# A two-layer hybrid trunk on one core: weights loaded and accumulated in halves of a unit, 47 instead of 55 accumulations, 137 units split whole, a new order of the items, zero matmuls at the first gate

## What is computed

```
x += 1/2 * (silu(h @ w1) * (h @ w3)) @ w2        # h = RMSNorm(x)
P  = RMSNorm(x) @ W_in                           # one projection for all branches
A: retention, 4 heads;  B: window attention, 16 q / 2 kv heads;  C: attention into 256 memory tokens
y  = sum_b sigmoid(gate_b) * (branch_b @ W_up_b);  x += y @ W_o
x += 1/2 * (silu(h @ w1') * (h @ w3')) @ w2'     # h = RMSNorm(x)
```

## Time and profile before

| what | value |
|---|---|
| median of three executions | 1435.11 us (1435.1 to 1437.61) |
| the profiled execution | 1435.34 us |
| its span, first to last instruction | 1433.5 us |
| mean granted TensorE clock | 0.997 |
| PE, DVE, ACT, POOL busy | 99%, 84%, 69%, 4% |
| DMA | 336.14 MB, mean 234 GB/s |

### The profile page before, as it was taken

How to read it: one execution, slowest core, us unless ns; L and a number is a source line. 1 busy time by engine, 2 the same in 40 slices (tenths; PEclk the granted TensorE clock), 3 DMA queues, 4 the chain that set the end, 5 groups by cost and what they waited for, 6 DMA issues and landing times.

```text
span 1433.5 us, 17418 instructions
## 1 busy us (share of the span) xinstructions
PE 1415.2 (99%) x6630; PEld 1161.0 (81%) x6630; DVE 1205.6 (84%) x1423; ACT 982.2 (69%) x1438; POOL 63.3 (4%) x88
## 2 busy tenths in 40 slices
PE   8999999999999999999999999999999999999997
PEld 6788888877878888888888888887778788888886
DVE  7999756889899868899889997468998898699885
ACT  6677666878766748676577675667786766576773
POOL 0000000000100000000000000000001000000000
PEclk9999999999999999999999999999999999999999
DMA  9799448787777576889749767468878765857971
GB/s 369 235 268 291 189 157 289 226 240 209 217 227 256 185 294 245 240 272 276 247 155 285 247 195 263 171 241 261 237 208 223 250 220 187 322 151 250 314 225 44
DMA packets 48675, 336.14 MB, mean 234 GB/s; under 512 B 5488, under 2 KB 6128, under 8 KB 8528
## 3 DMA queue, kind: packets, MB, share of 16 engines
q1 hardware_dynamic: 37536, 259.80, 48.4%
q0 software_dynamic: 8192, 58.59, 21.5%
q10 hardware_dynamic: 2864, 16.64, 2.9%
HBM read 327.67 MB, written 7.34 MB: 234 GB/s over the span
## 4 chain that ended last, share of the span: by engine, by line
PE 89%; DVE 6%; DMA 2%; ACT 1%; issue 1%; SPq 0%; POOLq 0%; POOL 0%; DVEq 0%; ACTq 0%
PE bank L815 27%; PE bank L818 27%; PE bank L816 27%; PE bank L876 3%; DVE w_lo L1671 3%; DMA raw<-in_stream 2%; PE bank L1170 1%; PE bank L1149 1%; PE bank L1031 1%; PE bank L1045 1%; ACT w_hi L1250 1%; DVE raw_x L1663 1%; PE bank L1060 1%; DVE raw_q L1663 0%; DVE w_lo_more L1671 0%
## 5 line engine op out<-in xcount | busy, mean ns | idle before, releaser
L1671 DVE TENSOR_TENSOR w_lo<-raw,w_hi 128x1024 fp32r<-128x1024 f32 x328 | 386.2, 1221 | 104.3 <-ACT w_hi L1250 103.9
L1250 ACT ACTIVATE w_hi<-raw 128x1024 fp32r<-128x1024 f32 x328 | 328.5, 1054 | 141.0 <-PE bank L818 115.5
L815 PE MATMUL bank<-w_hi,hT_lo 128*128 128x512 f32 (+1 forms) x640 | 251.4, 393 | 3.3 <-ACT stA L1489 1.6
L818 PE MATMUL bank<-w_lo,hT_hi 128*128 128x512 f32 (+1 forms) x640 | 246.2, 385 | 0.0
L816 PE MATMUL bank<-w_hi,hT_hi 128*128 128x512 f32 (+1 forms) x640 | 246.1, 384 | 0.0
L815 PE MATMUL bank<-w_hi,S_lo 128*128 128x512 f32 x400 | 158.8, 397 | 0.9 <-ACT snap L1338 0.9
L818 PE MATMUL bank<-w_lo,S_hi 128*128 128x512 f32 x400 | 155.9, 390 | 0.0
L816 PE MATMUL bank<-w_hi,S_hi 128*128 128x512 f32 x400 | 155.9, 390 | 0.0
L815 PEld LDWEIGHTS bank<-w_hi,hT_lo 128*128 128x128 f32 x640 | 120.3, 188 | 32.0 <-issue 4.0
L818 PEld LDWEIGHTS bank<-w_lo,hT_hi 128*128 128x128 f32 x640 | 120.3, 188 | 24.4
L816 PEld LDWEIGHTS bank<-w_hi,hT_hi 128*128 128x128 f32 x640 | 120.5, 188 | 22.3
(11 more groups left out here) (232 smaller groups left out, 2529.6 us busy)
## 6 DMA issues: line engine op xcount, KB each, us to landing
raw<-in_stream SPq DMA_DIRECT2D x154, 1024.0 KB, 5.5
raw_b<-in_stream SPq DMA_DIRECT2D x35, 1024.0 KB, 6.9
raw_q<-in_stream SPq DMA_DIRECT2D x33, 1024.0 KB, 7.7
raw<-in_stream POOLq DMA_DIRECT2D x24, 1024.0 KB, 8.7
raw_x<-in_stream SPq DMA_DIRECT2D x16, 1024.0 KB, 5.2
raw_b<-in_stream POOLq DMA_DIRECT2D x10, 1024.0 KB, 10.8
raw_q<-in_stream POOLq DMA_DIRECT2D x9, 1024.0 KB, 9.0
raw_a<-in_stream SPq DMA_DIRECT2D x6, 1024.0 KB, 5.1
```

What stands on the lines that cost most here:

```text
L815: nc.tensor.matmul(dst, xl, wh[:, a:b], start=first, stop=False, skip_group_check=more)
L818: return nc.tensor.matmul(dst, xh, wl[:, a:b], start=False, stop=last, skip_group_check=more)
L1250: nc.scalar.activation(slots(o)[0][:, part], raw_slot(s)[:, part], ACT.Copy).then_inc(hi_split, 1)
L1671: nc.vector.tensor_tensor(lo[:, part], raw_slot(s)[:, part], hi[:, part].bitcast(F32), ALU.subtract)\
```

## The change

1. **Halves.** Each load by SP is two DMAs of 512 KB, and each slot has two semaphores. Where the slot becomes free with the end of a split, the first half is issued one count of `weights_made` earlier (`SPLIT_ENDS`), when the first half of the old unit has been split. Each accumulation by POOL is two DMAs too. ACT waits for each half by itself (`raw_there`).
2. **ADDED** has 47 sums in place of 55, and DVE makes 65 in place of 57.
3. **WHOLE** was empty. Now 137 of the 328 units that are split at L1250 and L1671 in either layer are copied and subtracted with one instruction of 128x2048 (the list has 162 entries, of which 25 name no item).
4. **The order tables** are new. PE's matmuls on weights stay the same in number and shape.
5. **warm** issues 8 matmuls of zeros (128x512) on PE into the bank of the first gate's transposes, once that bank is free and before PE waits for `act_g`.

```diff
-mk0.1+xt0 mk1.0+xt1 mk1.1 S_sum S_hi skv.0 S_lo sq1.0 sq0.0 sq0.1 mkt sq1.1 skt mv0.0 sqt rk:1 rk:5 s0 mv0.1
...
-gs:7 ro gs:4 mq:5 mq:1 us0.1 mq:3 re mq:6 us1.0 mq:2 mq:7 us1.1 mq:4 gr:1 mqt gr:5 rt mkT_in mv_in gr:3 gr:6
+gs:7 ro gs:4 mq:5 re us0.1 mq:1 mq:3 mq:6 us1.0 mq:7 mq:2 mq:4 us1.1 gr:1 mqt gr:5 rt mkT_in gr:3 gr:6 mv_in
...
 FFN_ORDER = {(0, 1): """
-u0.0 u0.1 u1.0 g0 u1.1 p0:1 d0 g1 p0:5 p0:3 p0:6 p0:2 d1 p0:7 p1:5 p0:4 g3 p1:3 p1:1 d3 p1:6 g2 p1:2 d2 p1:7
+u0.0 u0.1 u1.0 g0 u1.1 p0:1 d0 p0:5 p0:3 p0:6 g1 p0:2 d1 p0:7 p1:5 p0:4 g3 p1:3 p1:1 d3 p1:6 g2 p1:2 d2 p1:7
...
 """.split(), (1, 1): """
-u0.0 u0.1 u1.0 g0 p0:1 u1.1 d0 p0:5 p0:3 p0:6 g1 p0:2 p0:7 p1:5 d1 g3 p0:4 p1:3 p1:1 d3 p1:6 g2 p1:2 p1:7 p2:5
+u0.0 u0.1 p0:1 u1.0 g0 u1.1 d0 p0:5 g1 p0:3 p0:6 p0:2 p0:7 p1:5 d1 p0:4 g3 p1:3 p1:1 d3 p1:6 g2 p1:2 p1:7 d2
...
-S_AFTER = {(0, 1): (0, 0, 3, 0, 4, 4), (0, 2): (0, 1, 2, 0, 3, 5), (1, 1): (0, 2, 3, 0, 3, 3), (1, 2): (0, 2, 2, 1, 2, 5)}
+S_AFTER = {(0, 1): (0, 3, 3, 0, 3, 4), (0, 2): (0, 1, 1, 0, 2, 4), (1, 1): (0, 2, 3, 0, 2, 4), (1, 2): (2, 2, 2, 2, 3, 4)}
...
-    (0, 2, 1): (6, 7, 4), (0, 2, 2): (7,), (0, 2, 3): (6, 7), (0, 0, 'rk'): (7, 4), (0, 0, 'rg'): (6, 7, 4),
-    (0, 0, 'gs'): (6, 7), (0, 0, 'mq'): (6, 7, 4), (0, 0, 'gr'): (7,), (0, 0, 'gm'): (7,), (1, 1, 0): (7, 4),
+    (0, 2, 1): (6, 7), (0, 2, 2): (6, 7), (0, 2, 3): (7,), (0, 0, 'rk'): (7,), (0, 0, 'rg'): (6, 7, 4),
+    (0, 0, 'gs'): (7,), (0, 0, 'mq'): (6, 7), (0, 0, 'gr'): (7,), (0, 0, 'gm'): (7,), (1, 1, 0): (7, 4),
...
             for o, unit, s, (until, owner), _ in loads[EARLY:]:
                 if until > 0:
-                    sp.wait_ge(weights_made, until)
+                    sp.wait_ge(weights_made, until - (until in SPLIT_ENDS))
...
-                sp.dma_start(raw_slot(s), stream[unit]).then_inc(raw_loaded[s], 16)
+                for n, part in enumerate(PARTS):
+                    if n and until > 0 and until in SPLIT_ENDS:
+                        sp.wait_ge(weights_made, until)
+                    sp.dma_start(raw_slot(s)[:, part], stream[unit, :, part]).then_inc(raw_loaded[s][n], 16)
...
+                    for h, part in enumerate(PARTS):
+                        pool.wait_ge(raw_loaded[to[0]][h], 16 * to[1])
...
+                        pool.dma_start(raw_slot(to[0])[:, part], stream[l * NU + quarter_unit(f, k, SUMS[m]), :, part], accum_op=ALU.add)\
...
                     if c == 0 and (l, f) == (0, 1):
                         pe.wait_ge(x0_copied, 2)
+                        pe.wait_ge(*room(l, f"gt{f}_{c}"))
+                        warm(8, where[l][f"gt{f}_{c}"][0])
...
                 if whole(o):
+                    raw_there(1)
                     nc.scalar.activation(slots(o)[0][:, :], raw_slot(s)[:, :], ACT.Copy).then_inc(hi_split, 2)
                     return
-                for part in PARTS:
+                for n, part in enumerate(PARTS):
+                    if n:
+                        raw_there(1)
```

More of the change, by code:

```diff
@@ L510, in sem @@
             return ctx.enter_context(nc.semaphore(name))
-        raw_loaded = [sem(f"raw_loaded{s}") for s in range(RAW_A + 1)]
+        raw_loaded = [[sem(f"raw_loaded{s}_{n}") for n in range(2)] for s in range(RAW_A + 1)]
         hi_split, weights_made, unit_used = sem("hi_split"), sem("weights_made"), sem("unit_used")
@@ L515, in build @@
         S_step, x0_copied = sem("S_step"), sem("x0_copied")
-        quarter_added = {m: [sem(f"quarter_added{m}_{n}") for n in range(2)] for m in (5, 6, 7, 4)}
+        quarter_added = {m: [[sem(f"quarter_added{m}_{n}_{h}") for h in range(2)] for n in range(2)] for m in (6, 7, 4)}
         x_stored, x_back, mkT_stored, mkT_back, mv_stored, mv_back = map(
@@ L614, in pair_no, with sum_ready @@
             return l * (len(PAIRS[1]) + len(PAIRS[2])) + (f - 1) * len(PAIRS[1]) + k
-        def sum_ready(l, pair, k):
+        def sum_ready(l, pair, k, h):
             if k in added(l, pair):
                 turn, count = (added_at[l, pair, k] - 1) % 2, (added_at[l, pair, k] + 1) // 2
-                return quarter_added[k][turn], 16 * count
+                return quarter_added[k][turn][h], 16 * count
             return weights_made, sum_at[l, pair, k]
@@ L676, in x_part @@
                 sp.dma_start(x[:, :, cols], x_in[:, cols].rearrange("(t p) d -> p t d", p=P)).then_inc(x_loaded[n], 16)
+            SPLIT_ENDS = {v for v in lo_at if v}
             x_part(0)
@@ L735, in add_quarters @@
                     to = raw_of[l, pair, WEIGHT[m]]
-                    pool.wait_ge(raw_loaded[to[0]], 16 * to[1])
-                    if behind:
-                        pool.wait_ge(weights_made, behind)
                     _, f, k = pair
-                    pool.dma_start(raw_slot(to[0]), stream[l * NU + quarter_unit(f, k, SUMS[m])], accum_op=ALU.add)\
-                        .then_inc(quarter_added[m][(added_at[l, pair, m] - 1) % 2], 16)
+                    for h, part in enumerate(PARTS):
+                        pool.wait_ge(raw_loaded[to[0]][h], 16 * to[1])
+                        if behind:
+                            pool.wait_ge(weights_made, behind)
+                        pool.dma_start(raw_slot(to[0])[:, part], stream[l * NU + quarter_unit(f, k, SUMS[m]), :, part], accum_op=ALU.add)\
+                            .then_inc(quarter_added[m][(added_at[l, pair, m] - 1) % 2][h], 16)
             def quarters_after(l, i):
@@ L790, in _, with warm @@
                 pe.nop().then_inc(psum_free[b], 1)
-            def warm(n):
+            def warm(n, b=0):
                 for _ in range(n):
-                    nc.tensor.matmul(ps[0][:, :], still[:, 0:P], still[:, :], start=True, stop=True)
+                    nc.tensor.matmul(ps[b][:, :], still[:, 0:P], still[:, :], start=True, stop=True)
             pe.wait_ge(still_ready, 1)
@@ L1237, in split, with raw_there @@
                 s, loads_so_far = loaded(o)
-                if item[0] == "prod" and item[3] in SUMS:
-                    act.wait_ge(*sum_ready(l, item[:3], item[3]))
-                else:
-                    act.wait_ge(raw_loaded[s], 16 * loads_so_far)
+                def raw_there(h):
+                    if item[0] != "prod" or item[3] not in SUMS:
+                        act.wait_ge(raw_loaded[s][h], 16 * loads_so_far)
+                    elif item[3] in added(l, item[:3]) or h == 0:
+                        act.wait_ge(*sum_ready(l, item[:3], item[3], h))
+                raw_there(0)
                 if slot_before[o] >= 0:
@@ L1658, in split @@
                     to, plus = (raw_of[o // NI, pair, q] for q in (WEIGHT[m], SUMS[m]))
-                    dve.wait_ge(raw_loaded[to[0]], 16 * to[1])
-                    dve.wait_ge(raw_loaded[plus[0]], 16 * plus[1])
+                    for n in range(2):
+                        dve.wait_ge(raw_loaded[to[0]][n], 16 * to[1])
+                        dve.wait_ge(raw_loaded[plus[0]][n], 16 * plus[1])
                     if sum_behind[o // NI, pair, m]:
```

27 lines of the change are left out of this document (14 added, 13 removed), and 8 rows, old and new, of the table ADDED.

## The result

The change makes the kernel slower: the median is 1448.26 us (1445.98 to 1450.04, four executions) against 1435.11, a ratio of 1.0087 with a 95% interval of 1.0075 to 1.0099. 1430.7 was forecast. The profiled execution took 1449.13 us, its span is 1447.3.

The account below looks back on a forecast made before the run. PE, busy 99%, was taken as the bound, with DVE limiting the first 70 us. Terms -1.65 - 2.1 - 0.9 - 0.4 - 0.2 + 0.6 = -4.65 gave 1430.7 us; 8-in-10 range 1428.2 to 1434.8.

Parts of the forecast that it names:

- loads and accumulations in halves: All transfers: less load on the queues and no PE wait for loads after 70 us; 0, bounds -0.5 and +1 us.
- The margin at us0.1: Narrowest place for DVE's added sums: first half of w_lo ready 0.5 us before PE takes it up.
- Whole splits: DVE: one full instruction replaces a pair of half splits, 0.07 us saved each; nine in the first 70 us give -0.6.
- one such place: A stall like that possible at us0.1, where a whole split comes 1.2 us later; +0.6 us, bounds 0 and +3.
- The mixing stages: Both layers: gr:1 finds bank 0 free, -2.1 us; rt's wait for `mqT` goes, -0.9 us.
- if something else is late there, 0: Upper bound of the gr:1 term in the mixing stage: the -2.1 us gain could come to nothing.
- rival 2: Only part holds: full DVE in the mixing stage brings waits back, 1433.2 us; or start fails, 1432.4; 0.21 shared with another rival.
- Rival 3: Slower: six DVE sums come due in the mixing stages, 1.7 us each, 10.2 in all, 1440.9 us; chance 0.09.
- The signs: Prediction wrong if PE waits over some 2 us for w_lo/w_hi after 70, p0:4 starts before 67.5, or whole-split cost differs clearly.
- The start: DVE's chain up to 70 us: earlier first half, whole splits and no idle for `act_b`, -1.65 us at p0:4.
- The zero matmuls: First gate: they hold the clock up, but DVE ends this stretch; 0, bounds 0 and -1.7 us.
- Rival 1: Start: the whole clock loss is won too, 1.7 us more, giving 1429.0 us; chance 0.20.

Follow-up runs that it names:

- all_one: The changed kernel with each load and each accumulation one DMA of 1 MB again; 1433.31 us, ratio 0.9982.
- all_one_no_whole: The changed kernel with loads and accumulations of 1 MB and an empty list of whole splits; 1431.93 us, ratio 0.9981.
- all_one_added55: The changed kernel with loads and accumulations of 1 MB and the 55 accumulations of the kernel before in place of 47; 1435.11 us, ratio 0.9999.
- before_warm: The kernel before with only the eight zero matmuls at the first gate added; 1435.49 us, ratio 1.0002.
- acc_rows: The kernel before with each accumulation in two DMAs of 512 KB cut by rows (64 rows of 8192 bytes), loads of 1 MB; 1453.10 us, ratio 1.0122.
- ffn_load_halves: The kernel before with the new order, sums and S_AFTER of the FFNs, the zero matmuls and loads in halves; 1432.93 us, ratio 0.9977.
- acc_one: The changed kernel with each of the 47 accumulations one DMA of 1 MB again, loads still in halves; 1437.72 us, ratio 1.0016.
- before_load_halves: The kernel before, with its tables and accumulations of 1 MB, and only the loads in halves; 1433.39 us, ratio 0.9991.

## Why the prediction was wrong

**The step that failed** is the one on loads and accumulations in halves: "PE waits for no load after 70 us, as the waits show, so I take 0. Bounds: -0.5 and +1". It is worth +15 us between all_one and the changed kernel, the share of the whole splits with late transfers included. By the ratios the loss is made up so: the new tables and the zero matmuls, with transfers of 1 MB and no whole split, gain 2.7 us; loads in halves then cost 4.2, accumulations in halves 4.3, and whole splits on top 6.7. In the tables of before, accumulations in halves cost 4.3 us as well on top of loads in halves, but loads in halves gained 1.3. So the new tables lose nothing by themselves and yet have a part in the loss, through the loads. Two things were wrong in the step. It took the cost of a transfer from the engines' time for its bytes; with 8 accumulations fewer that falls. But what counts is when the last half lands, and that is 2.4 us later at the median over all 55 (8.9 to 11.3 us, same tables). It goes with the traffic beside it: of the five accumulations in each of these two kernels beside which the other queues carried under 0.1 MB, the median went from 8.1 us only to 8.4. At 43.6 us the second half of the changed kernel lands 8.3 us after the first issue, as the whole did at 44.1. And it read from the list of waits that there is room, where the list only says that the room is not negative. The margin at us0.1, 0.5 us, stood in the prediction, but as one against added sums.

**Whole splits** were counted as -0.07 us each. Their price per instruction is right (2.28 to 2.29 us at L1681 from start to end, 2.20 from start to start in DVE's chain, and PE's loss is nothing clear with accumulations of 1 MB), but they cost 7 us together with late accumulations. The prediction priced the 1.2 us that the first half comes later, and then counted one such place.

**The mixing stages**, -2.1 and -0.9 us, failed as well. In layer 0 the new order with transfers of 1 MB gains 0.4 us from rg:7 to gr:2, and in layer 1 0.1. These are one execution's; in that of all_one_no_whole the same stretches lose 1.9 and gain 2.1. The wait for bank 0 does go, as forecast, and so does most of that for `mqT`. What I named as the bound "if something else is late there, 0" was the case: DVE, 90% busy, gives its combinations later, and PE waits at mq:7, mq:2 or mq:4 instead. The prediction itself had this as rival 2, with a split as what PE would wait for instead.

**Rival 3** (9%) named the right stages and the right sign, but its 1440.9 us is 7 us short, and its cause is not borne out: with transfers of 1 MB, taking eight sums back from DVE gains nothing (all_one_added55). Beside transfers in halves this wasn't run. So the 9% were on the right side by luck more than by their reason.

**The signs.** One of the prediction's signs of being wrong came: PE waits for `w_lo` after 70 us for 2.4 us in all (1.9 at L1681, 0.5 at L1686), against "some 2". It is the smaller part: of the 5.4 us for `gates` 4.1 are the two stops at gr:7 behind late accumulations, which no sign named.

**What held.** The start: -1.65 us were forecast at p0:4, -1.45 measured, with the forecast waits for `S_lo` (about 1.1; 1.0 measured, between starts less 0.23) and `gT2_lo` (1.4; 1.3) inside the stretch. p0:4 starts at 68.69 us (about 68.3 forecast). Nine splits up to there are whole, as counted; in the rows of Place 2 it is two pairs that become single, not three. The zero matmuls: 0, with the clock at 1.00 and the time handed to the next wait for DVE. Rival 1 thus falls. The Trainium skill (TensorE: Matmul & The Clock Gate, Part 1) has the clock follow how busy PE has been. before_warm agrees, with a granted clock of 1.00 where it was 0.51, and shows too that here it is worth nothing. Of the other page cited (DMA: Bandwidth & Descriptors, Bandwidth), the direction of the rule holds for the accumulations: halves of 1 MB were worse. The fixed 2.0 us stand in that page's section Anatomy of one DMA — SWDGE (gpsimd) path, as a fit to DMAs that GpSimd issues. A second one doesn't show where an accumulation has the queues almost to itself (0.3 us at the median); over all 55, two DMAs take 2.4 us more than one. For loads the rule doesn't decide: in halves they gained 1.3 us in one set of tables and lost 4 to 5 in another.

**Open.** Why two accumulating transfers land later than one when other queues are busy: acc_rows shows only that the size of the packets alone is not it. Why loads in halves cost 4.4 us with the new tables was not followed to a single place. With the new FFN tables and the old mixing stage they cost nothing (ffn_load_halves), so it lies with the mixing stage's tables. In acc_one's column above 3.8 us are lost in layer 0 between rg:7 and gr:2, where all_one gains 0.4. With loads in halves accumulations of 1 MB also land later, at a median of 9.3 us in acc_one against 8.7 in all_one and of 9.6 in before_load_halves against 8.9 in the kernel before, though in the latter it cost nothing.
